# Multiply-adds in fixed quanta, context rows scaled in place, a column-wise read-back, and low rotated keys in all rows, in a four-layer transformer kernel

## The reference, cut to what matters

```python
mod = silu(c) @ w_mod[l] + b_mod[l]; shift, scale, gate = split(mod, 3)      # c_ctx likewise: cshift, cscale, cgate
h  = rmsnorm(x,  norm_g[l]) * (1 + scale)  + shift                           # layers 0 and 1
hc = rmsnorm(cx, norm_g[l]) * (1 + cscale) + cshift
u = h @ w_in;  y = concat(mixer1(u, uc), mixer2(u, uc)) * silu(ug)
x = x + gate * (y @ w_o[l]);  cx = cx + cgate * (yc @ w_o[l])                # cx in layer 0 only
# layer 0: a (differential attention, 8 heads of 2 x 64) and b (windowed, 8 heads of 128, with a sink)
# layer 1: c (grouped heads of 128, q and k normed) and d (latent attention:
#          q = [q_nope 128, rope(q_pe) 64], k = [k_nope 128, rope(k_pe) 64], scores q . k / sqrt(192))
# then final_g norm, and layers 2 and 3 (mixers e, f, g, h) without modulation, and a last norm:
return rmsnorm(x, norm_f)
```

## Time and profile before

| | |
|---|---|
| median of 3 runs | 2457.74 us |
| profiled execution | 2459.69 us, its span 2457.9 us |
| TensorE matmuls | 2375.6 us busy, 97% |
| VectorE | 1526.6 us, 62% |
| ScalarE | 1034.1 us, 42% |
| GpSimd (POOL) | 232.2 us, 9% |
| DMA | 467.97 MB, mean 190 GB/s |
| mean granted clock | 0.994 |

### The profile page before, as it was taken

How to read it: one execution, slowest core, us unless ns; L and a number is a source line. 1 busy time by engine, 2 the same in 40 slices (tenths; PEclk the granted TensorE clock), 3 DMA queues, 4 the chain that set the end, 5 groups by cost and what they waited for, 6 DMA issues and landing times. The chain is left out here.

```text
span 2457.9 us, 31447 instructions
## 1 busy us (share of the span) xinstructions
PE 2375.6 (97%) x11660; PEld 1913.7 (78%) x11660; DVE 1526.6 (62%) x2575; ACT 1034.1 (42%) x1712; POOL 232.2 (9%) x329
## 2 busy tenths in 40 slices
PE   6999999999899999998999999999999999999998
PEld 1587778877677878887777788978888888898886
DVE  1367766777677867757746666676576544444654
ACT  3322333334343322333453445445454545664543
POOL 0001010011010000001121100100110001101100
PEclk9999999999999999999999999999999999999999
DMA  9957544444334465666475465866655577667653
GB/s 370 360 183 258 177 146 154 150 141 142 108 120 138 162 235 168 197 196 228 142 234 151 125 204 162 263 204 193 202 171 186 180 212 225 184 194 246 185 192 127
DMA packets 231175, 467.97 MB, mean 190 GB/s; under 512 B 17642, under 2 KB 42536, under 8 KB 229744
## 3 DMA queue, kind: packets, MB, share of 16 engines
q1 hardware_dynamic: 209104, 394.94, 49.8%
q0 software_dynamic: 21920, 71.01, 9.1%
HBM read 435.10 MB, written 30.79 MB: 190 GB/s over the span
## 5 line engine op out<-in xcount | busy, mean ns | idle before, releaser
L2120 PE MATMUL pp<-w_hi,hT_hi 128*128 128x512 f32 (+3 forms) x2904 | 1168.2, 402 | 9.4 <-DVE w_lo L1520 3.9
L2122 PE MATMUL pp<-w_hi,hT_lo 128*128 128x512 f32 (+3 forms) x2904 | 1115.2, 384 | 0.0
L2121 PE MATMUL pp<-w_lo,hT_hi 128*128 128x512 f32 (+3 forms) x2904 | 1113.0, 383 | 0.0
L1520 DVE TENSOR_TENSOR w_lo<-raw,w_hi 128x1024 fp32r<-128x1024 f32 (+4 forms) x568 | 669.3, 1182 | 562.4 <-ACT w_hi L1240 561.0
L1240 ACT ACTIVATE w_hi<-raw 128x1024 fp32r<-128x1024 f32 (+4 forms) x568 | 578.6, 1023 | 452.2 <-PE pp L2122 378.1
L2120 PEld LDWEIGHTS pp<-w_hi,hT_hi 128*128 128x128 f32 x2904 | 547.0, 188 | 137.3 <-issue 35.0
L2122 PEld LDWEIGHTS pp<-w_hi,hT_lo 128*128 128x128 f32 x2904 | 545.9, 188 | 105.1
L2121 PEld LDWEIGHTS pp<-w_lo,hT_hi 128*128 128x128 f32 x2904 | 547.7, 189 | 95.1 <-issue 7.5
L1620 DVE SCALAR_TENSOR_TENSOR arena<-raw,cT,arena 128x512 f32<-128x512 f32 x240 | 172.4, 745 | 1.0 <-issue 0.3
L1620 DVE SCALAR_TENSOR_TENSOR xy<-raw,cT,xy 128x512 f32<-128x512 f32 x180 | 126.8, 745 | 0.0
L1401 ACT ACTIVATE arena<-pY 128x512 f32<-128x512 f32 (+2 forms) x114 | 62.1, 544 | 148.9 <-PE pY L2281 116.2
(11 more groups left out here) (311 smaller groups left out, 1749.2 us busy)
## 6 DMA issues: line engine op xcount, KB each, us to landing
raw<-in_w_in_dram SPq DMA_DIRECT2D x168, 512.0 KB, 4.3
raw<-in_w_mod_dram SPq DMA_DIRECT2D x158, 512.0 KB, 5.0
raw<-in_e_w_in_dram SPq DMA_DIRECT2D x102, 512.0 KB, 4.7
raw<-in_w_o_dram SPq DMA_DIRECT2D x64, 512.0 KB, 4.7
raw<-in_o_w_in_dram SPq DMA_DIRECT2D x64, 512.0 KB, 5.0
raw<-in_w_out_dram SPq DMA_DIRECT2D x64, 512.0 KB, 3.9
raw<-in_w_in_dram SPq DMA_DIRECT2D x56, 440.0 KB, 4.0
scratch_u<-ust POOLq DMA_DIRECT2D x35, 512.0 KB, 4.3
```

The costliest lines, as they stand in the source:

```text
L1520: dve.tensor_tensor(w_lo[:, g.s % SPLIT, 0:n], raw_of(g)[:, 0:n], w_hi[:, g.s % SPLIT, 0:n].bitcast(F32), ALU.subtract).then_inc(lo_done, 1)
L2120: pe.matmul(dst, hT_hi[:, kk, o:o + P], hi[:, k, :], start=a, stop=False)
L2121: pe.matmul(dst, hT_hi[:, kk, o:o + P], lo[:, k, :], start=False, stop=False)
L2122: ins = pe.matmul(dst, hT_lo[:, kk, o:o + P], hi[:, k, :], start=False, stop=z)
```

## The change: what it does, and the diff

- `beside` has no credit any more. `room(slot)` says how many multiply-adds a slot takes: from slot 100 to 164 one or two in turn, then one for twelve slots, then one in two of four slots (0 and 2 of each b unit; 0 and 3 of each a unit, counted from its score), from y0_3 on one or two in 24 of each 32 slots (none in the four or so on either side of a chunk's end), none around the start of c_q0, then two of four. The late chunks take a fourth and a fifth accumulator in turn; folds stand at least four slots behind a chunk's last multiply-add (two before). By this table the last multiply-add before layer 1 is at slot 583 (590 before), and those of gate1 are at 612 to 737 (597 to 723 before). LEAD is 3, was 4.
- The context rows are scaled in place by ScalarE (`ctx_scale`, four instructions at slots 612 and 613) and then transposed; the diagonal remains for the x rows.
- `reload` is four steps of 512 columns (slots 461, 469, 477, 491), each with its own semaphore; a residual add waits for its own columns.
- `copy` for b and `finish` for a are on ScalarE, not VectorE.
- `kpe_lo` has all 128 rows, and L2262 uses the whole q_pe. The score gains the product of the two low parts.
- out3_3 is ordered tokens-first; sum, power, gain and output scaling go by token tile; stores are two of 1024 columns for tile 0, four of 512 for tile 1. ScalarE scales columns 0 to 1023 of tile 0 and 0 to 511 of tile 1, VectorE the rest.

```diff
-LEAD = 4
+LEAD = 3
+    def room(self, slot):
+        C = self.C
+        b0, a0 = C["a_q0"].q0 + 4, C["a_q0"].q0 + 148
+        if slot < b0:
+            return 1 + slot % 2
+        if slot < b0 + 12:
+            return 1
+        if slot < a0:
+            return (slot - b0) % 4 in (0, 2)
+        if slot < C["y0_3"].q0:
+            return (slot - a0) % 4 in (0, 3)
+        if slot < C["out0_3"].q1 - 7:
+            p = (slot - C["y0_3"].q0) % 32
+            return 4 < p < 29 and 1 + (p % 5 in (1, 3))
+        if slot < C["c_q0"].q0 + 4:
+            return 0
+        return (slot - C["c_kv"].q1) % 4 in (0, 1)
...
-        rate = [(C["b_q1"].q0 + 4, 1.0), (C["b_kv"].q0, 1.4), (C["a_q0"].q0 + 14, 0.65), (C["y0_0"].q0 + 24, 0.55), (C["y0_3"].q0, 1.0), (C["c_q0"].q0, 0.5)]
...
+            late = ch.name.startswith("gate1")
+            ch.lanes = (0,) if late else (0, 1)
+            if late:
+                slot, used = max(slot, self.sides[i - 1].macs_end + (9 if self.sides[i - 1].row is None else 1)), 0
...
+                for K, v in itertools.product(g.ks, ch.lanes):
+                    while used >= self.room(slot):
+                        slot, used = slot + 1, 0
+                    used += 1
...
         for g in last:
-            for t in (2, 3):
+            for t in range(ch.T // 2, ch.T):
                 self.quantum(g, t)
...
+            self.run(ch, upto=5 if n == 3 else None)
+        self.tokens_first(ch, (5, 6, 7))
...
-        add(last.q1 + 11, "reload")
+        for n, s in ((2, last.groups[1].q1 + 5), (3, last.groups[3].q1 + 5), (0, last.groups[5].q1 + 5), (1, last.q1 + 11)):
+            add(s, "reload", n)
...
-        add(q1 + 4, "diag", 2, 4)
+        for n in range(2):
+            add(q1 + 4 + n, "ctx_scale", 2, n)
+            add(q1 + 4 + n, "ctx_scale", 3, n)
...
+        for t in range(2):
+            q = C["out3_3"].end[t]
+            add(q + 2, "sums", "f2", t)
+            add(q + 2, "root", "f2", t)
+            for n in range(4):
+                add(C[f"out3_{n}"].end[t] + (2 if n < 3 else 1 + t), "x_gain", t, n)
+                add(q1 + 2 + t, "x_out", t, n)
...
-            first, second = [s for s in free if s >= ch.macs_end + 2][:2]
+            first, second = [s for s in free if s >= ch.macs_end + 4][:2]
...
-        kpe_hi, kpe_lo, qpe = hT_hi[:, 14:16, 256:512], hT_lo[0:64, 14:16, 256:512], hT_hi[:, 12:14, 256:512]
+        kpe_hi, kpe_lo, qpe = hT_hi[:, 14:16, 256:512], hT_lo[:, 14:16, 256:512], hT_hi[:, 12:14, 256:512]
-        accs = [xy[:, 0:2, 512:1024], xy[:, 2:4, 512:1024], b_mask]
+        accs = [xy[:, 0:2, 512:1024], xy[:, 2:4, 512:1024], b_mask, at(5632, 2, 512), at(8704, 1, 512)]
...
+            for t, c, w, n_act, n_dve in ((0, 0, 1024, 2, 0), (0, 1024, 1024, 2, 2), (1, 0, 512, 3, 2), (1, 512, 512, 3, 3), (1, 1024, 512, 3, 4), (1, 1536, 512, 3, 5)):
+                sp.wait_ge(out_act, n_act)
+                if n_dve:
+                    sp.wait_ge(out_dve, n_dve)
+                sp.dma_start(out[0][P * t:P * t + P, c:c + w], xy[:, t, c:c + w]).then_inc(out_here, 16)
...
+                if m == "c" and n == 0:
+                    pool.wait_ge(*folded(C["shift1_3"]))
...
+            def reload(n):
+                for K in range(4 * n, 4 * n + 4):
...
+                pool.dma_start(xy[:, 0:2, cols], D["x"][0][:, cols].rearrange("(t p) n -> p t n", p=P)).then_inc(x_again[n], 16)
+                pool.dma_start(xy[:, 2:4, cols], D["ctx"][0][:, cols].rearrange("(t p) n -> p t n", p=P)).then_inc(x_again[n], 16)
...
+            def ctx_scale(t, n):
+                act.wait_ge(rooted, nth["root", "n1", 1])
+                x = xy[:, t, 1024 * n:1024 * n + 1024]
+                act.activation(x, x, ACT.Copy, scale=rs[:, RS["n1"] + t:RS["n1"] + t + 1]).then_inc(x_scaled, 1)
...
+            def finish(m, n, u):
+                if m != "a":
+                    return
+                x = plan.U[m, n, u]
+                act.wait_ge(probed, prob_n[x.key])
+                act.wait_ge(filled["O"], left["O", ("pv", *x.key)])
+                c0 = MIX["a"].ycol + 128 * n
+                act.activation(xy[:, x.qt, c0:c0 + 128], pO[:, 0:128], ACT.Copy, scale=rl[:, x.i % 4, 0:1]).then_inc(freed["O"], 1)
...
-                dve.tensor_tensor(kpe_lo, pY[0:64, :].rearrange("p (k n) -> p k n", k=2), kpe_hi[0:64].bitcast(F32), ALU.subtract).then_inc(freed["Y"], 1)
+                dve.tensor_tensor(kpe_lo, pY[:, :].rearrange("p (k n) -> p k n", k=2), kpe_hi.bitcast(F32), ALU.subtract).then_inc(freed["Y"], 1)
...
+                elif l == 1 and t0 == 2:
+                    pe.wait_ge(x_scaled, 4 + nth["ctx_scale", 3, K // 8])
+                    for k in range(2):
+                        for t in range(2):
+                            ins = pe.transpose(b[:, 256 * k + 128 * t:256 * k + 128 * t + 128], xy[:, t0 + t, 128 * (K + k):128 * (K + k) + 128], ident)
...
-                        ins = pe.matmul(b[:, 0:w], q_pe[0:64], kpe_lo, start=False, stop=True)
+                        ins = pe.matmul(b[:, 0:w], q_pe, kpe_lo, start=False, stop=True)
```

More of the change, by code:

```diff
@@ L185, in run @@
             self.put(ch, j)
-    def rate(self, table, slot):
-        return [r for s, r in table if s <= slot][-1]
+    def room(self, slot):
[15 more added lines that the diff above has]
+        return (slot - C["c_kv"].q1) % 4 in (0, 1)
     def beside(self):
         C = self.C
-        rate = [(C["b_q1"].q0 + 4, 1.0), (C["b_kv"].q0, 1.4), (C["a_q0"].q0 + 14, 0.65), (C["y0_0"].q0 + 24, 0.55), (C["y0_3"].q0, 1.0), (C["c_q0"].q0, 0.5)]
-        free_b, taken_a = C["a_q0"].q0 + 152, C["y0_0"].q0 + 20
+        free_b, free_c, taken_a, taken_c = C["a_q0"].q0 + 152, C["y0_0"].q0 + 92, C["y0_0"].q0 + 20, C["c_q0"].q0 + 40
         self.macs = []
-        slot, credit = rate[0][0], 0.0
+        slot, used = C["b_q1"].q0 + 4, 0
         for i, ch in enumerate(self.sides):
-            lanes = (0,) if ch.name.startswith("gate1") else (0, 1)
-            ch.lanes = lanes
-            ch.mac0 = slot
+            late = ch.name.startswith("gate1")
+            ch.lanes = (0,) if late else (0, 1)
+            if late:
+                slot, used = max(slot, self.sides[i - 1].macs_end + (9 if self.sides[i - 1].row is None else 1)), 0
+            elif i and slot + 4 > taken_a:
+                same = [p for p in self.sides[max(0, i - 2):i] if p.acc == (3 if i % 2 == 0 and slot > free_c else 2)]
+                if same and same[-1].macs_end + 9 > slot:
+                    slot, used = same[-1].macs_end + 9, 0
             for j in range(KT_ // GROUP):
@@ L205, in beside @@
                 self.sided.append(g)
-                while credit < 0:
-                    credit += self.rate(rate, slot)
-                    slot += 1
-                for i_, (K, v) in enumerate(itertools.product(g.ks, lanes)):
+                for K, v in itertools.product(g.ks, ch.lanes):
+                    while used >= self.room(slot):
+                        slot, used = slot + 1, 0
+                    used += 1
                     g.macs.append(slot)
                     self.macs.append((slot, ch, K, v))
-                    pair = self.rate(rate, slot) > 1 and i_ == 1
-                    credit += 0 if pair else self.rate(rate, slot)
-                    slot += 0 if pair else 1
-                credit -= len(g.macs)
                 g.q0 = g.macs[0]
-            ch.macs_end = g.macs[-1]
-            ch.acc = i % 2
-            if ch.macs_end + 8 > taken_a:
-                assert ch.mac0 > free_b, (ch.name, ch.mac0, free_b)
-                ch.acc, slot, credit = 2, max(slot, ch.macs_end + 7), 0.0
+            ch.mac0, ch.macs_end = ch.groups[0].macs[0], g.macs[-1]
+            if late:
+                ch.acc = 2 + 2 * (i % 2)
+            elif ch.macs_end + 9 < taken_a:
+                ch.acc = i % 2
+            elif i % 2 == 0 and ch.mac0 > free_c and ch.macs_end + 9 < taken_c:
+                ch.acc = 3
+            else:
+                ch.acc = 2
+                assert ch.mac0 > free_b
         n = 0
@@ L236, in tokens_first @@
             last.append(g)
-            for t in (0, 1):
+            for t in range(ch.T // 2):
                 self.quantum(g, t)
         for g in last:
-            for t in (2, 3):
+            for t in range(ch.T // 2, ch.T):
                 self.quantum(g, t)
@@ L559, in schedule @@
         add(C["out3_0"].q0, "gain_row", 2)
-        add(q1 + 2, "sums", "f2", 0)
-        add(q1 + 2, "root", "f2", 0)
-        for n in range(4):
-            q = C[f"out3_{n}"].q1
-            add(q + 2, "x_gain", 0, n)
-            add(q + 2, "x_gain", 1, n)
-            add(q1 + 4, "x_out", 0, n)
-            add(q1 + 4, "x_out", 1, n)
+        for t in range(2):
[5 more added lines that the diff above has]
+                add(q1 + 2 + t, "x_out", t, n)
     def beside(self):
@@ L1220, in _ @@
                     elif name == "reload":
-                        reload()
```

(11 more changed lines are left out.)

56 lines of the change are left out of this document (24 added, 32 removed).

## The result

The changed kernel takes 2418.86 us (median of 4 runs, 2417.01 to 2420.02), the kernel before 2457.72 beside it: ratio 0.984, interval 0.9828 to 0.9851, so 38.9 us less. The forecast was 2434, a gain of 23.6. Direction right, size too small, and outside the range on record (2422 to 2449).

A forecast was written before the change was run, and what follows sets the result against it. TensorE, busy 97% of the span, was taken as the bound, so only less work or fewer waits could help. Terms 6.2 + 3.8 + 3.0 + 8.0 + 2.5 - 1.0 + 1.1 = 23.6 us gave 2434 us, range 2422 to 2449.

The forecast's parts named there:

- Part 1: The 16 d scores: without the 64-row matmul each unit takes 1.55 us instead of 1.94; gain 6.2 us.
- Rival (c): d scores: the tiling-mode drain accounts for all excess distance, so 11.2 us go there; 2429 us, chance 0.05.
- Part 2: Context turns: transposes replace diagonal products, ScalarE's scalings mostly covered, gate1 fold moved away; gain 3.8 us.
- Part 3: Output product of layer 0: multiply-adds kept away from chunk ends remove residual-add waits; gain 3.0 us.
- Part 4: a heads: finish on ScalarE and fixed multiply-add slots cut waits and low clock, 10.5 less 2.5 given back; gain 8.0.
- Part 5: b stretch: the copy moved to ScalarE removes two waits of TensorE; gain 2.5 us.
- Part 6: Layer 1 fronts: later gate1 puts seven more multiply-adds beside late front copies; loss 1.0 us.
- Part 7: End: token tile 0 finishes three quanta earlier, so its first store goes sooner; gain 1.1 us.
- Rival (d): a heads: two fixed multiply-adds per unit fall into the closed chain, some 20 us slower; 2478 us, chance 0.05.
- Rival (b): Whole kernel: all named waits go and nothing is given back, 33.4 us; near 2424 us, chance 0.08.
- (a): Whole kernel: only the work shrinks and waits return elsewhere, gain 10.1 us; 2448 us, chance 0.17.
- (e): Whole kernel: little does what it says (64 rows cost nothing, banks late), about 3 us; 2455 us, chance 0.07.

The follow-up runs named there:

- e5: Kernel before with only the low keys in all rows, context rows scaled in place and the reordered end: 2452.0 us.
- e4: Kernel before with only the new placement of multiply-adds (room, five accumulators, folds from +4, LEAD 3): 2448.18 us.
- e7: Kernel before with only the reload of x and ctx in four column pieces: 2455.04 us.
- e8: Kernel before with only the b copy and the a finish moved to ScalarE: 2452.84 us.
- e3: Changed kernel with the b copy back on VectorE: 2420.81 us.
- e13: Kernel before with only LEAD 3 in place of 4: 2450.77 us, ratio 0.9969.
- e1: Changed kernel with the old placement of multiply-adds (credit and rate, three accumulators, folds from +2, LEAD 4): 2435.87 us, ratio 0.9918.
- e6: Changed kernel with x and ctx reloaded whole at slot 491 instead of in column pieces: 2426.45 us.
- e2: Changed kernel with the a finish back on VectorE: 2426.34 us.
- e9: Changed kernel with the weight splits of the a stretch one slot later, behind the probabilities: 2412.82 us.
- e11: Changed kernel with LEAD 4 again, all else new: 2438.1 us in the only run.
- e10: Changed kernel with the front copies of mixer c on ScalarE: 2419.24 us.
- e15: Changed kernel with LEAD 2 in place of 3: 2419.32 us.

## Why the prediction was right in direction and too small

Gain by stretch, forecast and measured:

```
part                      forecast   measured (span)   by itself
1 keys                       6.2         6.39           e5 6.39
2 context rows               3.8         4.66           e5 1.63, e4 1.19
3 output product             3.0         5.65           e7 2.41, e4 -2.16
4 a heads                    8.0        13.87           e8 7.69, e4 8.19
5 b copy                     2.5         4.33           e3 1.7,  e4 2.60
6 gate1, fronts             -1.0         5.11           e13 6.86
7 end                        1.1         1.42           e5 1.01
y0_3 and start                0         -0.80
```

**Part 1 right**, to 0.2 us: 1.56 us per unit for 1.55 forecast. The Trainium skill, "TensorEngine Tiling (Array Packing)", Key Properties, says that changing the tiling mode drains TensorE; the trace agrees in kind (with the 64-row matmul gone the three distances are 0.09, 0.20 and 0.09 us shorter), but whether it is a drain or the 64-row matmul itself that cost them no run tells apart. Rival (c), which read all distances above 0.23 us as drain, is refuted: L2309 to L2310 is still 0.63 us with 128 rows on both sides, so that excess follows the float32 matmul, as the row of mixer b had said.

**Part 2 right in its sum, wrong in its cover.** The cover of ScalarE's four scalings held: they take 4.4 us (4.1 forecast), and no split is late in c_q0. What I costed at 0.7, the gate1 fold, is worth more once the transposes are faster (1.8 us wait in e5); moving it away is what makes the edit whole.

**Part 3: the cause holds only together with the columns, and the term was too small.** I put the 3.0 us down to multiply-adds between residual adds, and the columns down to a part of the longest wait (1.7). The columns alone give 2.4 and leave 1.0 us of these waits (e7); with the columns in, the placement takes the last of them and 3.3 us in all (e1 against after); but the placement without the columns makes the stretch 2.2 us longer (e4). The step that failed is "so that only a quarter is late", followed to the residual adds and POOL's queue and not to the weights it competes with: the transfer of the whole reload delays a *weight* group by some 6 us on the full DMA engines (e6), and with the new placement a fold stands behind it.

**Part 4: two steps wrong in opposite ways.** The 3.0 us for eleven L1889 waits, each shorter by 0.27, did not come: with the finish away they are still 7.5 us (e8); only with the new placement does the finish take 1.4 off them (5.6 in e2, 4.2 after). Of the 7.7 us that e8 does gain, 5.9 are in the rows of waits (the L1401 waits 4.0, the folds 1.8), and the 39 distances into bank Y fall by 5.3 us, their median from 0.36 to 0.23: the rest is in delays too short for the rows. The 1.7 for the clock is not in it, for e8 still has its piece at 1.2 GHz; e4, e7 and after have none in this stretch, and e7 prices it at 1.5. And "I give back 2.5" was not seen: the placement takes another 6.3 on top (after against e1), 3.4 of it off the probabilities' wait (7.6 in e1, 4.2 after). The closed chain had slack to give, since w_lo stood ahead of the probabilities: e9, which moves only the splits, removes the 4.2 us that were left of this wait in a stretch that shrinks by 7.3. No part of the prediction weighed that order.

**Part 5**: the copy itself gives 1.7 (forecast 2.5); the other 2.6 of the stretch are the placement's (e4), which I had costed at 0 outside the places named.

**Part 6 and LEAD: the steps that failed.** "LEAD 3 loads a group a quantum later; L1620 is never seen waiting for its data, so 0" asked about the loads that are moved back, not those that are thereby moved forward. SyncE's queue is strict: a side load waits for its slot (51.3 us in all in 200 to 262 us of e11), and the weights behind it wait too. Measured: 7.6 us for before (e13), 19.2 for after (e11). And for the fronts I foresaw a loss of 1.0 through later multiply-adds, and a gain of 5.1 was measured. The slots given for gate1 ahead of the prediction were wrong as well: taken from the plan of the new kernel, gate1 runs in slots 595 to 721 and the last multiply-add before layer 1 in 586, not 612 to 737 and 583, so there are no "seven more": 34 of them stand in the slots of the fronts where 32 did. What the 5.1 us are made of is known in part. TensorE's waits there are 14.0 us before, 11.8 in e1, 10.1 in e13 and 9.4 after, and the pieces of 1.2 GHz two, one, none and one. LEAD alone takes 3.9 us of waits (e13); but e1, which has LEAD 4 and the other edits, already gains 3.95 us of stretch, so the two overlap, and about 1.2 us of after's 5.1 is clock.

**Part 7 right.** The stores start 1.2 us sooner after the last matmul; the end is 1.4 shorter.

Rival (d), multiply-adds inside the closed chain, did not appear: no wait for a maximum came up. Rival (b), all waits gone and nothing given back, was nearest (2424), and the result lies beyond it, because its bounds held nothing for LEAD or for a gain in the fronts. Its 14 us for the a stretch, which no sum in the text gives, were met (13.9) by luck. There TensorE's waits fell by 9.2 us (16.0 to 6.8) and the clock gave 1.5; the other 3.2 are in what the rows of waits leave out. Two slips change nothing that follows: the "14.6 elsewhere" of rival (d) is 23.6 - 8.0 = 15.6, and the 0.70 of part 1's upper bound is 0.69.

Rivals (a) and (e), that waits come back, are refuted by the same rows; the one wait that is longer in after (1.9 us in y0_3 for 0.9, for bank O, which a fold's reduction frees) costs 1.2, and it is 0.8 or 0.9 in e4, e6, e10 and e15, so it may not belong to the change. Open: what decides whether a wait is followed by a piece of low clock; no run holds the clock fixed.

## What to carry to other kernels

In a strict load queue ask of every reordering what moves *forward*: a side load that waits for a ring slot holds all weights behind it, and two engines later that shows as a fold or a front that is late, with its name on another cause. Try the one-number knobs of such an order (LEAD, the slot of a split) on the chip before placing work by hand: LEAD 3 alone gave 7.6 us, and one slot on the splits of the a stretch 7.3 us there, more than the hand placement of all multiply-adds did (6.3). And test such a knob together with the placement: with LEAD 4 the placement gave nothing, with LEAD 3 11.8 us. Where waits go, count the low clock behind them as well and the delays that are too short for a row of waits (sum the distances from start to start), and don't subtract an allowance for a chain that will be met again without a row that shows it.

## What the runs showed of the hardware that I had not expected

The granted clock fell to 1.2 GHz for 3.4 us (or for 6.8, as in e4, e6 and e11) behind waits of TensorE, but not behind each. In the fronts, with the same three waits, it followed the one of 1.9 us in after (low from 1132.7 us) and not those of 2.3 and 2.1 us; in e2 it followed the latter two (2.3 and 2.2 us there, low from 1172.1 and 1209.7) and not the first. At 1.2 GHz the starts of successive matmuls are 0.43 us apart instead of 0.23 (e11), and 3.4 us of it cost 1.5 us in the a stretch (before against e7) and 1.2 in the fronts (e2 against after). The piece in the fronts of after, clock third from the right:

```profile
1132.70:1136.10 3.40, 3.40 (x15) 3.40 (x16) 1.29 (x3) 0.36 (x1) 0.00 (x0) 0.50 0.55 154
```

A bulk read of 4 MB beside the weight stream raised the DMA share to 1.03 for 15 us (0.90 in after) and put one weight group of 512 KB back by 6 us (843.95 to 850.03, e6); in pieces of a quarter, issued from 784 to 835 us, it cost nothing that TensorE saw.
